# A SwiGLU layer with its gate and up products taken by blocks: low parts on VectorE alone, the norm's factor through PSUM, the second pair's first products brought forward, and the planes of the down product interleaved

## The reference, cut to what matters

```python
x = x + mix @ swa_w_out                      # attention's output projection
h = x * rsqrt(mean(x * x, -1) + 1e-6) * norm_ffn
gu = h @ w_gate_up                           # 1024 x (2 * 2816)
x = x + (silu(gu[..., :2816]) * gu[..., 2816:]) @ w_down
out = x * rsqrt(mean(x * x, -1) + 1e-6) * final_norm
```

## Time and profile before

| | us |
|---|---|
| median of 3 runs (lowest, highest) | 2247.53 (2244.11, 2251.00) |
| the profiled execution | 2245.76 |
| its span, first to last instruction | 2243.9 |
| TensorE busy in the span | 2063.4 (92%) |
| VectorE, ScalarE, GpSimd busy | 1409.5, 965.0, 651.8 |

### The profile page before, as it was taken

The page is one execution under the profiler, slowest core; times in us unless marked ns, Lnnn a source line. Parts: engine busy times, 40 slices in busy tenths (PEclk is TensorE's granted clock), DMA queues, the critical chain, the costliest instruction groups (busy, mean ns, idle before and its releaser), DMA issues. The chain is left out here.

```text
span 2243.9 us, 44558 instructions
## 1 busy us (share of the span) xinstructions
PE 2063.4 (92%) x15672; PEld 1547.2 (69%) x15672; DVE 1409.5 (63%) x1797; ACT 965.0 (43%) x1459; POOL 651.8 (29%) x468
## 2 busy tenths in 40 slices
PE   5999989896688999979789989898899999989998
PEld 4788867686344555545478867686788888868887
DVE  7888638525577888868657268458655655543154
ACT  5212157202577888868531057424433333311023
POOL 1433311220000000000125622136555555523253
PEclk8999999997799999989879999999999999999999
DMA  7643123317999699999832300121222222243133
GB/s 284 229 157 124 39 88 129 134 57 299 396 421 421 245 396 422 422 422 422 343 145 75 99 1 1 38 84 38 76 84 84 84 84 84 93 160 112 63 104 125
DMA packets 93078, 397.41 MB, mean 177 GB/s; under 512 B 10220, under 2 KB 21324, under 8 KB 68044
## 3 DMA queue, kind: packets, MB, share of 16 engines
q1 hardware_dynamic: 73708, 353.95, 41.6%
q10 hardware_dynamic: 13968, 23.07, 2.8%
q0 software_dynamic: 5328, 19.40, 2.2%
HBM read 351.24 MB, written 45.14 MB: 177 GB/s over the span
## 5 line engine op out<-in xcount | busy, mean ns | idle before, releaser
L1710 PE MATMUL moe_hu<-x_res,acc_sq 128*32 128x256 f32 x5120 | 318.5, 390 | 25.8 <-DVE acc_sq L1629 14.6
L1607 DVE COPY x_res<-moew_raw 128x2048 f32 x243 | 269.4, 1136 | 107.3 <-PE moe_hu L1710 52.0
L1710 PEld LDWEIGHTS moe_hu<-x_res,acc_sq 128*32 128x32 f32 x5120 | 159.5, 112 | 144.1 <-issue 35.7
L1607 ACT ACTIVATE x_res<-moew_raw 128x2048 f32 (+1 forms) x121 | 197.9, 1635 | 39.6 <-DMA moew_raw<-in_w 21.9
L1618 ACT ACTIVATE moe_wdown<-moew_raw 128x2048 f32 x80 | 153.4, 1917 | 38.8 <-PE moe_y L1721 33.2
L1721 PE MATMUL moe_y<-moe_wdown,moe_at 128*32 128x256 f32 x2560 | 154.8, 383 | 2.2 <-ACT moe_at L1755 2.2
L2542 PE MATMUL ff_bank<-xh,ff_u_hi 128*128 128x512 f32 x352 | 138.9, 394 | 13.4 <-ACT ff_sq L2648 8.8
L1667 POOL COPY moew_idx<-rows 128x1 int32 (+1 forms) x20 | 11.9, 595 | 460.5 <-PE moe_xturn L1693 460.5
L2500 POOL TENSOR_TENSOR ff_u_lo<-ff_raw,ff_u_hi 128x512 fp32r<-128x512 f32 x66 | 90.8, 1376 | 179.8 <-ACT ff_u_hi L2638 179.7
L2542 PE MATMUL ff_bank<-xl,ff_u_hi 128*128 128x512 f32 x352 | 137.7, 391 | 0.0
L2542 PE MATMUL ff_bank<-xh,ff_u_lo 128*128 128x512 f32 x352 | 137.5, 391 | 0.0
(11 more groups left out here) (483 smaller groups left out, 4820.3 us busy)
## 6 DMA issues: line engine op xcount, KB each, us to landing
moew_raw<-in_w SPq DMA_DIRECT2D x192, 1024.0 KB, 16.1
ff_raw<-in_w_up SPq DMA_DIRECT2D x44, 512.0 KB, 3.6
mid_w_raw<-in_w_qkv SPq DMA_DIRECT2D x24, 512.0 KB, 3.6
in_w_raw<-in_w_in SPq DMA_DIRECT2D x23, 512.0 KB, 3.6
a_scratch<-x_res SPq DMA_DIRECT2D x44, 256.0 KB, 2.3
ff_sums<-a_scratch SPq DMA_DIRECT2D x22, 512.0 KB, 4.3
xbc<-in_w_ada SPq DMA_DIRECT2D x20, 512.0 KB, 8.0
y_scratch<-moe_ysb ACTq DMA_DIRECT2D x80, 128.0 KB, 6.9
```

Of the source, the lines that this page charges most:

```text
L1607: m = e.activation(to, src, ACT.Copy) if k == "act" else e.tensor_copy(to, src)
L1710: m = e.matmul(hu[u % 2][rows(j), 0:2 * FW].rearrange("p (a f) -> p a f", a=2), xt[:, t, rows(u)], w[:, :, FW * j:FW * (j + 1)], start=(t ...
```

## The change

1. **Low parts of the borders on VectorE alone.** GpSimd made three low parts of t2 and four of t4; VectorE makes them now, t2 and t3 in one instruction of 128x2048 each. All of t4 comes after b22.
2. **The last square** (`square(KT - 1)`, `add_square(KT - 1)`) moves back: on ScalarE behind t4's high parts, on VectorE behind pair 0's first gate sum.
3. **The norm's factor by token sums.** TensorE makes eight 128x1 sums into PSUM, VectorE and ScalarE take the reciprocal and the root of 128x8 values (`rt`), VectorE multiplies them into a block diagonal (`diag`, 128x1024), and TensorE spreads it with the matrix of ones into PSUM (`total`), where it stays: `by_root` reads PSUM instead of SBUF.
4. **The order on TensorE.** Pair 1's product 0 comes ahead of pair 0's product 6, pair 1's product 1 behind it; the token sums come then, the spreading comes between pair 1's products 3 and 4. ScalarE's and VectorE's programs for pairs 0 and 1 follow that order. Pair 1 is written out, the loops start at pair 2.
5. **Two buffers for `up22`**, by turns.
6. **Planes later.** On VectorE planes 0 and 1 stand ahead of pair 21's work, plane 2 behind its corner, plane 3 behind its second gate sum; on ScalarE two planes and one gate by turns. TensorE waits for `act_done` of pair 21 ahead of the first part's second tile (it writes the bank that holds the factor). In the later parts the addition of the finished tile comes before `plane_low`, and the queue waits for the last stores behind the first plane of the second part, not ahead of it.

The diff, cut to its core:

```diff
                     for t in range(LASTP * KT):
                         n, j = t // KT, t % KT
-                        if t < K2:
-                            e.dma_start(x[:, t, :], self.xs_dram[t]).then_inc(s_kept[t], 16)
                         if j < FF_PARTS[n + 1]:
                             load_plane(first_plane[n + 1] + j)
                         load_down(t + 4)
+                        if t == 0:
+                            for h in range(2):
+                                for b in range(2):
+                                    e.wait_ge(s_stored[h][b], 16 * (NPR // 2) + 16)
+                        if t < K2:
+                            e.dma_start(x[:, t, :], self.xs_dram[t]).then_inc(s_kept[t], 16)
...
-                    for k in range(3):
-                        st.wait(e, st.act, "h_t2")
-                        st.pool(e.tensor_tensor(xl[:, k, A], x[:, k, B], xh[:, k, A].bitcast(F32), ALU.subtract), f"l_t2{k}")
-                    for k in range(K2):
-                        st.wait(e, st.act, f"h_t4{k}")
-                        st.pool(e.tensor_tensor(gl4[:, k, :], x[:, k, B], gh4[:, k, :].bitcast(F32), ALU.subtract), f"l_t4{k}")
...
+                    product(q0, 0, 5, lambda k: st.wait(e, st.dve, f"l_b22{k}"))
+                    product(q1, 1, 0)
+                    c22.wait(e, q0)
+                    product(q0, 0, 6, lambda k: st.wait(e, st.dve, f"l_t4{k}"))
+                    product(q1, 1, 1)
                     st.wait(e, st.dve, f"added{KT - 1}")
+                    for t in range(NT):
+                        m = e.matmul(total[0][:, t:t + 1], acc_sq[:, t * P:(t + 1) * P], self.const("ones")[:, 0:1], start=True, stop=True)
+                    st.pe(m, "square_sums")
+                    kept.wait(e, q1, 1)
+                    product(q1, 1, 2)
+                    product(q1, 1, 3)
+                    st.wait(e, st.dve, "diag")
                     for h in range(2):
-                        m = e.matmul(total[h], self.const("ones"), acc_sq[:, span(h)], start=True, stop=True)
-                    st.pe(m, "total")
-                    product(Q(0), 0, 3, lambda k: st.wait(e, st.dve, f"l_b21{k}"))
-                    kept.wait(e, Q(0), 3)
-                    product(Q(0), 0, 4, lambda k: st.wait(e, st.dve, f"l_t3{k}"))
-                    kept.wait(e, Q(0), 2)
-                    product(Q(0), 0, 5, lambda k: st.wait(e, st.dve, f"l_b22{k}"))
-                    c22.wait(e, Q(0))
-                    product(Q(0), 0, 6, lambda k: st.wait(e, st.pool, f"l_t4{k}"))
+                        m = e.matmul(total[h], self.const("ones"), rstd[:, span(h)], start=True, stop=True)
+                    st.pe(m, "root_spread")
+                    kept.wait(e, q1, 3)
+                    product(q1, 1, 4)
+                    kept.wait(e, q1, 2)
+                    product(q1, 1, 5)
+                    c22.wait(e, q1)
+                    product(q1, 1, 6)
...
                         for b in range(2):
+                            if n == 0 and b == 1:
+                                act_done.wait(e, LAST, 1)
+                                scaled.wait(e, pair_at(LAST, -1), 1)
```

ScalarE:

```diff
                     for k in range(K2):
                         st.act(e.activation(xh[:, K2 + k, B], half(K2 + k, 1), ACT.Copy, scale=norm_w(K2 + k)), f"h_b22{k}")
+                    high(q1, 0)
                     for k in range(K2):
                         st.wait(e, st.dve, f"t4{k}")
                         st.act(e.activation(gh4[:, k, :], half(k, 1), ACT.Copy), f"h_t4{k}")
-                    for p in range(6):
-                        high(Q(1), p)
+                    square(KT - 1)
+                    high(q1, 1)
+                    prod.wait(e, q1, 1)
+                    step.wait(e, q0, 1)
+                    keep_as(q1, 1, 0)
+                    for p in range(2, 6):
+                        high(q1, p)
+                    prod.wait(e, q1, 2)
+                    c22.wait(e, q0)
+                    keep_as(q1, 1, 1)
                     st.wait(e, st.dve, "inverse")
-                    st.act(e.activation(rstd[:, :], rstd[:, :], ACT.Sqrt), "rstd")
+                    st.act(e.activation(rt[:, :], rt[:, :], ACT.Sqrt), "root")
                     e.preload_act_table(ACT.Silu)
+                    prod.wait(e, q1, 3)
+                    step.wait(e, q0, 2)
+                    keep_as(q1, 1, 2)
+                    prod.wait(e, q1, 1)
+                    high(q1, 6, after=False)
                     for h in range(2):
-                        gate(Q(0), 0, h)
...
-                    for m in range(FF_PARTS[0]):
-                        plane_high(m, 0, m)
                     for h in range(2):
+                        for m in (2 * h, 2 * h + 1):
+                            plane_high(m, 0, m)
                         gate(LAST, 1, h)
```

VectorE:

```diff
-                    st.dve(lower(xl[:, 3, A], half(3, 1), xh[:, 3, A]), "l_t23")
-                    add_square(KT - 1)
+                    st.dve(lower(xl[:, 0:K2, A], x[:, 0:K2, B], xh[:, 0:K2, A]), "l_t2")
...
+                    st.wait(e, st.dve, "l_t2")
+                    for k in range(K2):
+                        st.dve(less(half(k, 1), half(K2 + k, 0), norm_w(K2 + k), half(k, 1)), f"t4{k}")
+                    for k in range(K2):
+                        st.wait(e, st.act, f"h_t4{k}")
+                        st.dve(lower(gl4[:, k, :], half(k, 1), gh4[:, k, :]), f"l_t4{k}")
...
-                        act_done.wait(e, pair_at(q, -1), 2)
-                        c22.done(e.tensor_tensor(up22, XYZ[s][0], r5, ALU.add))
+                        act_done.wait(e, pair_at(q, -2), 2)
+                        c22.done(e.tensor_tensor(up22[s], XYZ[s][0], r5, ALU.add))
...
-                        out.done(e.tensor_tensor(t, t, rstd[:, span(h)], ALU.mult))
...
-                    st.wait(e, st.pe, "total")
+                    corner(q0, 0)
+                    sum_weights(q1, (0,))
+                    gate_sum(q0, 0, 0)
+                    add_square(KT - 1)
+                    sum_weights(q1, (1, 2, 3))
+                    gate_sum(q0, 0, 1)
+                    st.wait(e, st.pe, "square_sums")
+                    st.dve(e.tensor_scalar(rt[:, :], total[0][:, 0:NT], 1.0 / D, EPS, ALU.mult, ALU.add))
+                    st.dve.settle()
+                    st.dve(e.reciprocal(rt[:, :], rt[:, :]), "inverse")
+                    st.wait(e, st.act, "root")
+                    st.dve(e.tensor_tensor(diag, self.const("ident").unsqueeze(1).to_broadcast([P, NT, P]),
+                                           rt[:, :].unsqueeze(2).to_broadcast([P, NT, P]), ALU.mult), "diag")
+                    st.wait(e, st.pe, "root_spread")
                     for h in range(2):
-                        st.dve(e.tensor_scalar(rstd[:, span(h)], total[h], 1.0 / D, EPS, ALU.mult, ALU.add))
-                    st.dve.settle()
-                    st.dve(e.reciprocal(rstd[:, :], rstd[:, :]), "inverse")
-                    st.wait(e, st.act, "rstd")
+                        by_root(q0, 0, h, lambda: step.wait(e, q0, h + 1), scaled)
+                    corner(q1, 1)
                     for h in range(2):
-                        by_root(q, 0, h, lambda: step.wait(e, q, h + 1), scaled)
...
                         if more:
                             sum_weights(pair_at(q, 1))
+                        before(0)
                         gate_sum(q, s, 0)
                         by_root(q, s, 0, lambda: step.wait(e, q, 1), scaled)
-                        corner(q, s)
+                        if not cornered:
+                            corner(q, s)
+                        before(1)
                         by_root(q, s, 0, lambda: silu.wait(e, q, 1), step)
                         gate_sum(q, s, 1)
                         by_root(q, s, 1, lambda: step.wait(e, q, 3), scaled)
+                        before(2)
...
+                    def early_planes(n):
+                        for m in ((0, 1), (2,), (3,))[n]:
+                            plane_low(m, 0, m)
+                    pair(LAST, 1, more=False, before=early_planes)
...
                             gd.empty(e.tensor_tensor(x[:, j, :], gd.acc[t % 2][:, :], x[:, j, :], ALU.add))
+                            if t < FF_PARTS[n + 1]:
+                                plane_low(first_plane[n + 1] + t, n + 1, t)
```

142 lines of the change are left out of this document (67 added, 75 removed).

## The result

The changed kernel takes 2229.19 us, median of 4 runs (2224.34 to 2231.09), beside 2248.93 for the kernel before in the same series (2244.11 to 2251.00): a ratio of 0.9912, 95% interval 0.9889 to 0.9935. A second series of the same kernel gave 2230.76 and 0.9920 (0.9906 to 0.9934). The forecast was 2231.3, with a range from 2226 to 2239. It named a gain of 16.2 us where the medians give 19.7 and 17.3, so part of its nearness to 2229.19 is luck. The profiled execution took 2224.34 us (span 2222.5), 21.4 less than the one of before.

What follows compares the result with a forecast made beforehand. TensorE was taken as the bound, idle only at the pairs' two ends. Head 6.4 and tail 9.8 us off 2245.76 gave 2229.6 for the profiled execution, 2231.3 for the median, range 2226 to 2239.

Steps and rivals of the forecast that it cites:

- The bound: Last stage: TensorE, busy all 378.00 us in steady pairs, waits only at the pairs' two ends; only those can gain.
- the signs set down: Trace marks, e.g. two waits of 2.5 to 4 us at pair 2's products 1 and 2, b22's low parts 0.7 each.
- The borders: Head, pair 0: VectorE makes all low parts and the corner by 1554.4 us; product 6 waits 0.7 us.
- The factor: Head: token sums about 0.9 us, diagonal ready at about 1565.3 under two products, spreading 1.7 us.
- The chain to pair 2: Head: `act_done`, store, load, weight sums from 1580.0; idle 3.6 us twice, product 2 of pair 2 at 1589.4.
- the clock: Head, at pair 2's two waits: a fall to half clock priced at 1.8 us, bounds 0 and 3.0.
- The head: Pairs 0 and 1 up to pair 2: gain 8.2 us less 1.8 for the clock, 6.4 us, from 3.5 to 9.5.
- `by_root` from PSUM: VectorE: 0.69 us per step instead of 1.13; saves 35 us of busy time in steady pairs, TensorE nothing there.
- The tail: Pair 21 and first down parts: 7.9 us plus 1.9 us saved, 9.8 us, from 6.5 to 10.5.
- A: Rival, head gains nothing: `act_done` only 2 us earlier, stalls and clock eat it; gain 2 or less, 2236; chance 0.13.
- B: Rival, tail gains half: planes 2 and 3 wait for gates; gain 3 to 5, 2236 to 2237; chance 0.10.
- C: Rival, slower: `by_root`'s PSUM reads hold TensorE, 34 us lost, 2265; chance 0.06 with anything like it.

Runs made afterwards that it cites:

- the wide factor: Changed kernel with the norm's factor made as before: two large matmuls, reciprocal and root over 128x1024, `by_root` from SBUF; 2237.51 us, ratio 0.9959.

## Why the prediction was right, step by step

**The bound** was read rightly: steady pairs have no gap before or after, and all of the gain is at the two ends. Of the signs set down, two did not come: the waits at pair 2's products 1 and 2 are 1.90 and 1.72 us and not 2.5 to 4, and b22's low parts took 0.95 each and not 0.7.

**The borders** came as worked out. t2's low part took 2.29 us for the 2.31 from the slope of 0.54 per 512. By the Trainium skill's page "VectorE: DVE Perf Modes", section "The TRN2 errata", an fp32 tensor_tensor of 2048 would take 2.29, and the trace agrees. b22 took 3.81 (2.7 + 1), t4's low parts 2.48, and product 6 waited 0.49 for the corner (0.7 predicted; b22 and t4 add up to 1551.4 there and not 1551.1, which makes it 0.9). The run with the seventh product first shows the cover: without pair 1's product the wait is 3.19 (3.4 predicted).

**The factor.** The diagonal was ready 30.9 us after pair 0's start (30.7 predicted). Mis-sized were the square sums: 1.84 us and not 0.9, each of the eight being two instructions (x16 in the row).

**The chain to pair 2.** `act_done` came at 40.0 us after pair 0's start and not 39.0; the corner had stood 1.48 for TensorE's product 4, as foreseen, only that TensorE was 1.4 late by the square sums and a low part. But the load was issued 0.5 us after it and not 1.3, and landed 4.30 us after its issue and not 5.07. So the sums began at 44.8 (45.4 predicted), and as TensorE itself came 1.4 later, its wait was 1.9 and not 3.6. That the store holds the load, and that this chain is what is late next, the run with the load ahead confirmed: the first wait went.

**The step that failed in size is the clock.** The head gained 8.7 us and not 6.4. I had set down 1.8 us for a fall, as a cost on top of two waits of 3.6. The clock fell, for 8 matmuls. But it fell behind the first wait and was up again before the second, and so its 1.6 us only filled time that TensorE would have spent waiting for `ff_sq`: the second wait was 1.72. Here the slow clock ahead of a longer wait cost nothing, and behind the last long wait it cost in full, as the kernel with the load ahead showed with its 1.6. The other 0.5 us are in the chain: product 2 of pair 2 was due 54.8 us after pair 0's start and came at 54.3, the quicker issue and the shorter load having more than made good the later `act_done`. The load's part in that is luck: the same load took 4.17 to 5.29 us in the kernels here.

**`by_root` from PSUM** takes 0.684 us. The Trainium skill's rule on the port (page "SBUF — State Buffer", section "Who interferes with whom") says that a VectorE instruction with two SBUF inputs contends with a GpSimd instruction that reads SBUF, and one with a single SBUF input does not. Three rows bear it out: 0.684 with one SBUF operand, 1.04 with two in the same kernel otherwise, and 1.75 for weight sums beside GpSimd's t4. The 62 cycles more for a PSUM source that the Trainium skill's page "VectorE: DVE Perf Modes", section "The TRN2 errata", gives are not there: 0.684 from PSUM, 0.69 from SBUF where GpSimd is idle.

**The tail** gained 8.1 us within the stretch and 2.3 behind it, 10.4 against 9.8: the 0.4 and 0.7 of idle at product 6 and plane 3 did not come. The corner was done at 1958.4, 1.3 ahead of its product (1959.7), since planes 0 and 1 followed each other by 0.31 us of wait and not by 1.5 or more. The wait for a plane in the second part is 0.55 us and was an "issue" gap of 0.54 before.

**The rivals.** A (the head gains nothing) and B (half the tail) fell by the traces and by the two runs of one end each. C (PSUM reads hold TensorE) fell: 347.92 of 348 us busy in steady pairs, with some 74 such reads.

## What to carry to other kernels

A stall leaves its place in a queue: look at what stands behind the waiting instruction on its engine, and then move that, not the waiting one. Here the same two moves (a load ahead of a store, a corner behind the half that it delayed) gave 5 us more for a few lines, and the two runs that cost far more than expected (t4 on GpSimd, the wide factor) did so by the instruction behind. When two stalls follow each other, a slow clock between them costs only what the second stall doesn't cover; behind the last one it costs in full. And compare executions by a stretch that starts at the changed stage, since the stages ahead scatter by 10 us here.
